# Attention in units of four query heads, with scores in turns on the two row halves of TensorE and values in turns on its two column halves

## What is computed

```python
def _sink_attend(q, k, v, bias, sinks):
    s = jnp.einsum('bnqhgd,bnkhd->bnhgqk', q, k).astype(jnp.float32) * (HEAD_DIM_A ** -0.5) + bias
    sink = sinks.astype(jnp.float32).reshape(N_KV_A, GROUP_A)[None, None, :, :, None, None]
    m = jnp.maximum(jnp.max(s, axis=-1, keepdims=True), sink)
    p = jnp.exp(s - m)
    p = p / (jnp.sum(p, axis=-1, keepdims=True) + jnp.exp(sink - m))
    return jnp.einsum('bnhgqk,bnkhd->bnqhgd', p.astype(v.dtype), v)
...
x += W_out( sigmoid(g_A) * SWA(h) + sigmoid(g_B) * GLA(h) ),  h = RMSNorm(x)
x += SwiGLU(RMSNorm(x))
```

## Time and profile before

| | |
|---|---|
| three runs | 994.55, 994.57 (median), 995.9 us |
| span of the profiled execution | 994.7 us |
| TensorE matmuls busy | 959.4 us (96%) |
| VectorE busy | 469.1 us (47%) |
| ScalarE busy | 352.6 us (35%) |
| GpSimd busy | 325.3 us (33%) |
| TensorE's granted clock, mean | 0.999 |
| from first scores to last values | 296 to 524 us |

### The profile page before, as it was taken

The page is one execution under the profiler, slowest core; times in us unless marked ns, Lnnn a source line. Parts: engine busy times, 40 slices in busy tenths (PEclk is TensorE's granted clock), DMA queues, the critical chain, the costliest instruction groups (busy, mean ns, idle before and its releaser), DMA issues.

```text
span 994.7 us, 17842 instructions
## 1 busy us (share of the span) xinstructions
PE 959.4 (96%) x7171; PEld 897.7 (90%) x7171; DVE 469.1 (47%) x970; ACT 352.6 (35%) x661; POOL 325.3 (33%) x139
## 2 busy tenths in 40 slices
PE   3999999999889999999999999999999999999997
PEld 3899999988878787878789999999999999999997
DVE  5673656647777557776755344222113222122321
ACT  5542433434444444344434443222112222122231
POOL 2442312122222112222323334443334444334450
PEclk9999999999999999999999999999999999999999
DMA  8332213231222211121115222223223223323212
GB/s 228 88 84 64 75 53 65 53 75 51 69 65 64 64 43 43 52 56 43 43 29 168 86 85 86 84 84 105 86 80 89 84 84 91 91 77 90 65 55 68
DMA packets 148787, 76.34 MB, mean 77 GB/s; under 512 B 19280, under 2 KB 147622, under 8 KB 148726
## 3 DMA queue, kind: packets, MB, share of 16 engines
q1 hardware_dynamic: 142582, 71.88, 25.9%
q10 hardware_dynamic: 6144, 3.61, 1.3%
HBM read 71.87 MB, written 3.60 MB: 76 GB/s over the span
## 4 chain that ended last, share of the span: by engine, by line
PE 82%; DVE 12%; ACT 3%; issue 2%; DMA 1%; SPq 0%; ACTq 0%; DVEq 0%
PE G L487 23%; PE G L489 22%; PE G L488 22%; PE X L650 3%; PE X L621 2%; DVE qAT L1315 2%; PE X L634 2%; DVE den L1354 1%; DVE rs L1118 1%; DVE rs L1117 1%; DVE rt L1119 1%; DVE rv L1280 1%; DMA xtok<-in_x_sample_dram 1%; PE X L580 1%; ACT rs L894 1%
## 5 line engine op out<-in xcount | busy, mean ns | idle before, releaser
L465 POOL TENSOR_TENSOR w_lo<-wraw,w_hi 128x1024 fp32r<-128x1024 f32 x129 | 323.6, 2508 | 645.3 <-ACT w_hi L807 645.2
L487 PE MATMUL G<-h_hi,w_hi 128*128 128x272 f32 x1280 | 382.7, 299 | 11.0 <-DVE rv L1280 8.6
L489 PE MATMUL G<-h_hi,w_lo 128*128 128x272 f32 x1280 | 371.0, 290 | 0.0
L488 PE MATMUL G<-h_lo,w_hi 128*128 128x272 f32 x1280 | 369.0, 288 | 0.0
L487 PEld LDWEIGHTS G<-h_hi,w_hi 128*128 128x128 f32 x1280 | 241.6, 189 | 30.7 <-issue 28.0
L488 PEld LDWEIGHTS G<-h_lo,w_hi 128*128 128x128 f32 x1280 | 242.0, 189 | 0.6
L489 PEld LDWEIGHTS G<-h_hi,w_lo 128*128 128x128 f32 x1280 | 241.5, 189 | 0.0
L487 PE MATMUL G<-f_hi,w_hi 128*128 128x272 f32 x704 | 203.0, 288 | 0.0
L489 PE MATMUL G<-f_hi,w_lo 128*128 128x272 f32 x704 | 202.9, 288 | 0.0
L488 PE MATMUL G<-f_lo,w_hi 128*128 128x272 f32 x704 | 202.1, 287 | 0.0
L807 ACT ACTIVATE w_hi<-wraw 128x1024 fp32r<-128x1024 f32 x129 | 135.3, 1049 | 89.1 <-PE G L489 89.1
(11 more groups left out here) (217 smaller groups left out, 968.7 us busy)
## 6 DMA issues: line engine op xcount, KB each, us to landing
wraw<-in_w_in_dram SPq DMA_DIRECT2D x45, 512.0 KB
wraw<-in_w_gate_dram SPq DMA_DIRECT2D x22, 512.0 KB
wraw<-in_w_up_dram SPq DMA_DIRECT2D x22, 512.0 KB
wraw<-in_w_down_dram SPq DMA_DIRECT2D x16, 512.0 KB
xtok<-in_x_prompt_dram SPq DMA_DIRECT2D x8, 512.0 KB, 5.2
wraw<-in_w_in_dram SPq DMA_DIRECT2D x16, 256.0 KB
wraw<-in_w_out_dram SPq DMA_DIRECT2D x8, 512.0 KB
wraw<-in_w_down_dram SPq DMA_DIRECT2D x8, 384.0 KB
```

The lines of the kernel that those rows point to most:

```text
L465: pool.tensor_tensor(w_lo[:, slot, :, :], wraw[:, slot, :, :], w_hi[:, slot, :, :].bitcast(F32), ALU.subtract).then_inc(w_split, 1)
L487: pe.matmul(o, w_hi[:, slot, kc, :], b_hi[:, kc, cols], start=(kc == 0), stop=False)
L488: pe.matmul(o, w_hi[:, slot, kc, :], b_lo[:, kc, cols], start=False, stop=False)
L489: mm = pe.matmul(o, w_lo[:, slot, kc, :], b_hi[:, kc, cols], start=False, stop=(kc == last))
```

## The change

- **Units.** 20 units (group, token tile) of four heads in place of 40 of two. qA tile i now holds heads 2i (partitions 0 to 63) and 2i + 1 (64 to 127), and its weights come in one DMA instead of two.
- **Key copies.** kST and kcS hold the keys with the two halves of the partitions exchanged. Four DMAs from SBUF to SBUF on ScalarE's queue make them in `keys_out`, behind the two outputs of keys; a new semaphore `k_swapped` holds the first unit back until they have landed.
- **Scores.** Four matmuls in turn on rows 0 to 63 and 64 to 127, even heads into XB[0], odd heads into XB[1]. The scores wait for the maximum of the unit just before (they waited for the one two before).
- **Turns and values.** In two parts a = 0, 1 of two heads each. Each values matmul has one head (128 columns), in turn into partitions 0 to 63 and 64 to 127 of XB[3].
- **Places.** Unit u belongs to tile UNIT0 + u, one tile for four heads as before. Behind chunk 0: values (u - 2, 1) and scores u. Behind chunk 3: turn (u - 1, 0). Behind chunk 6: values (u - 1, 0) and turn (u - 1, 1).
- **Other engines.** One slot per tile, ahead of `read_out` and `gates`. ScalarE: four exponentials of u, then both copies of u - 1. VectorE: unit_out(u - 2) over all 128 partitions, unit_max(u), unit_scale(u).

```diff
-    tiles += [("qA", 4 * u + i, [(O_QA + (8 * u + i) * HD, HD), (O_QA + (8 * u + 4 + i) * HD, HD)])
-              for u in range(2) for i in range(4)]
+    tiles += [("qA", i, [(O_QA + i * P, P)]) for i in range(KC)]
...
-UNITS = [(g, j, par) for g in range(KV_A) for j in range(NJ) for par in range(2)]
+GH = HEADS_A // KV_A
+UNITS = [(g, j) for g in range(KV_A) for j in range(NJ)]
 NU = len(UNITS)
-NB = 4
-LAG_T, LAG_V = 3, 4
+NB = 2
+LAG = 2
...
             def unit_scores(u):
-                g, j, par, heads, nq, lo, hi = unit_shape(u)
+                g, j, nq, lo, hi = unit_shape(u)
                 if u == 0:
                     pe.wait_ge(kt_out, 1)
+                    pe.wait_ge(k_swapped, 16 * 4)
                     pe.wait_ge(norm_done, len(NORMS))
-                if u >= 2:
-                    pe.wait_ge(smax_ok, u - 1)
-                hf = slice((g % 2) * HD, (g % 2) * HD + HD)
+                if u >= 1:
+                    pe.wait_ge(smax_ok, u)
                 t0 = TOK[j][0]
...
+                for a in range(2):
+                    for par in range(2):
+                        hf = slice(par * HD, (par + 1) * HD)
+                        keys, old = (kAT, kcT) if g % 2 == par else (kST, kcS)
+                        q = qAT[hf, 2 * g + a, t0:t0 + nq]
+                        o = XB[par][0:nq, a * 2 * P:(a + 1) * 2 * P]
...
+                            mm = pe.matmul(o[:, lo:hi], q, keys[hf, g // 2, t0 - P + lo:t0 - P + hi],
+                                           start=True, stop=True)
...
-            def unit_values(u):
...
+            def unit_values(u, a):
+                g, j, nq, lo, hi = unit_shape(u)
+                pe.wait_ge(pt_copied, 2 * u + a + 1)
+                if a == 0 and u >= 1:
                     pe.wait_ge(oa_ok, u)
...
-                    mm = pe.matmul(o, v, probT[0:nk, u % 2, :, kt, 0:nq], start=(kt == lo // P), stop=(kt == 1))
+                    for par in range(2):
+                        mm = pe.matmul(XB[3][par * HD:(par + 1) * HD, a * P:a * P + nq], v,
+                                       probT[0:nk, a, par, kt, 0:nq], start=(kt == lo // P), stop=(kt == 1))
...
-            for u in range(NU + LAG_V):
-                n, k = UNIT0 + u // 2, 3 + 4 * (u % 2)
+            for u in range(NU + LAG):
+                n = UNIT0 + u
+                if u >= LAG:
+                    put(n, 0, unit_values, u - LAG, 1)
                 if u < NU:
-                    put(n, k, unit_scores, u)
...
+                    put(n, 0, unit_scores, u)
+                if 1 <= u <= NU:
+                    put(n, 3, unit_turn, u - 1, 0)
+                    put(n, 6, unit_values, u - 1, 0)
+                    put(n, 6, unit_turn, u - 1, 1)
...
                 act.dma_start(nk_s[0, 0].rearrange("t h d -> t (h d)"), kout[0:DEC, 1, :]).then_inc(out_sem, 16)
+                for dst, src in ((kST, kAT), (kcS, kcT)):
+                    act.dma_start(dst[0:HD, :, :], src[HD:P, :, :]).then_inc(k_swapped, 16)
+                    act.dma_start(dst[HD:P, :, :], src[0:HD, :, :]).then_inc(k_swapped, 16)
...
             def slot(u):
 
-                if LAG_T <= u < NU + LAG_T:
-                    unit_copy(u - LAG_T)
                 if 0 <= u < NU:
                     unit_exp(u)
+                if 1 <= u <= NU:
+                    unit_copy(u - 1, 0)
+                    unit_copy(u - 1, 1)
...
-                if 1 <= u <= NU:
-                    unit_scale(u - 1)
+                if LAG <= u < NU + LAG:
+                    unit_out(u - LAG)
                 if 0 <= u < NU:
                     unit_max(u)
-                if LAG_V <= u < NU + LAG_V:
-                    unit_out(u - LAG_V)
+                    unit_scale(u)
```

More of the change, by code:

```diff
@@ L197, in mixer_program @@
         kcT = tensor(mix, "kcT", [P, 2, P])
+        kST = tensor(mix, "kST", [P, 2, T])
+        kcS = tensor(mix, "kcS", [P, 2, P])
         vA = tensor(mix, "vA", [P, NJ, KV_A * HD])
@@ L342, in mixer_program @@
         kt_out = sem("kt_out")
+        k_swapped = sem("k_swapped")
         out_sem = sem("out_sem")
@@ L613, in unit_scores @@
                 t0 = TOK[j][0]
-                for a, head in enumerate(heads):
-                    q = qAT[hf, 4 * (g // 2) + head % 4, t0:t0 + nq]
-                    o = XB[u % 2][0:nq, a * 2 * P:(a + 1) * 2 * P]
-                    if j == SJ:
-                        pe.matmul(o[:, 0:P], q, kcT[hf, g // 2, :], start=True, stop=True)
-                        mm = pe.matmul(o[:, P:P + DEC], q, kAT[hf, g // 2, SEQ:T], start=True, stop=True)
-                    else:
-                        mm = pe.matmul(o[:, lo:hi], q, kAT[hf, g // 2, t0 - P + lo:t0 - P + hi],
-                                       start=True, stop=True)
+                for a in range(2):
[4 more added lines that the diff above has]
+                        o = XB[par][0:nq, a * 2 * P:(a + 1) * 2 * P]
+                        if j == SJ:
+                            pe.matmul(o[:, 0:P], q, old[hf, g // 2, :], start=True, stop=True)
+                            mm = pe.matmul(o[:, P:P + DEC], q, keys[hf, g // 2, SEQ:T], start=True, stop=True)
+                        else:
+                            mm = pe.matmul(o[:, lo:hi], q, keys[hf, g // 2, t0 - P + lo:t0 - P + hi],
+                                           start=True, stop=True)
@@ L623, in unit_scores, with unit_turn @@
                 mm.then_inc(qk_done, 1)
-            def unit_turn(u):
-                g, j, par, heads, nq, lo, hi = unit_shape(u)
+            def unit_turn(u, a):
+                g, j, nq, lo, hi = unit_shape(u)
                 pe.wait_ge(prob_ok, u + 1)
-                if u >= 1:
-                    pe.wait_ge(pt_copied, u)
-                for a in range(2):
+                if 2 * u + a >= 1:
+                    pe.wait_ge(pt_copied, 2 * u + a)
+                for par in range(2):
@@ L1017, in _ @@
                     act.preload_act_table_set(EXP_TANH)
-                slot(2 * (n - UNIT0))
+                slot(n - UNIT0)
                 if n == N_IN - 1:
@@ L1032, in _ @@
                     high_part(n + RING)
-                slot(2 * (n - UNIT0) + 1)
                 for h in range(HEADS_B):
@@ L1355, in unit_scale @@
                 link(dve.reciprocal(rd[0:nq, s, :], den[0:nq, s, :]))
-                for a in range(2):
-                    o = prob[0:nq, s, a, lo:hi]
-                    ins = dve.tensor_scalar(o, o, rd[0:nq, s, a:a + 1], 0.5, ALU.mult, ALU.mult)
+                for i in range(GH):
+                    o = prob[0:nq, s, i, lo:hi]
+                    ins = dve.tensor_scalar(o, o, rd[0:nq, s, i:i + 1], 0.5, ALU.mult, ALU.mult)
                 ins.then_inc(prob_ok, 1)
             def unit_out(u):
-                g, j, par, heads, nq, lo, hi = unit_shape(u)
-                dve.wait_ge(pv_done, u + 1)
+                g, j, nq, lo, hi = unit_shape(u)
+                dve.wait_ge(pv_done, 2 * (u + 1))
                 for i in (2 * g, 2 * g + 1):
```

83 lines of the change are left out of this document (38 added, 45 removed).

## The result

The changed kernel takes 965.7 us (median of 4 runs, 964.3 to 966.7) against 994.6 for the kernel before beside it: a ratio of 0.9706, 95% interval 0.9692 to 0.9719. Forecast were 971.0 us, 967 to 985. The span, from which the forecast was added up, went from 994.7 to 964.8 us.

A forecast was written before the change was run, and what follows sets the result against it. TensorE, busy 96% of the span, was taken as the bound. Span 994.7 - 26.0 (two halves at once) + 2.3 (late first scores) + 1.8 (lower clock) - 1.8 (wait on unit_out gone) = 971.0 us, range 967 to 985.

The forecast's parts named there:

- the sign: Whole kernel: the change makes it faster, chance 0.89; same 0.03, slower 0.08.
- the full overlap of both kinds: TensorE's scores and values: both array halves work at once, halving 27.9 and 24.3 us of passes, together -26.0 us.
- the hole: TensorE ahead of the first scores: 3.6 us idle waiting for the query tile, +2.3 us.
- the fall of the clock: TensorE after the idle time ahead of the first scores: clock at 1.2 GHz for 3 to 6 us, +1.8 us.
- the end of the wait on gaT: TensorE's wait for VectorE's unit_out: gone since unit_out comes seven chunks ahead of the values needing it, -1.8 us.
- B: Scores and values: partial overlap, 8 passes take 5 steps and not 4, giving 977.5 us; chance 0.12.
- C: Scores and values: only one of the two kinds overlaps, giving 983 or 985 us; chance 0.15.
- E: Scores and values: each change of half costs a 0.09 us drain, no overlap, giving 1011.8 us; chance 0.08.
- the zero of the serial work: TensorE's attention blocks: without overlap, passes, changes of kind (8 a tile) and first weights cost the same, 0 us.
- The margin of 0.5 us: Values at chunk 6: probT's chain through VectorE and ScalarE takes 4.93 us, TensorE 5.43, so no wait.
- rival D: Values at chunk 6: full overlap, but probT late by 0.5 us in each of 20 units, giving 981 us; chance 0.10.
- The key copies: ScalarE's queue behind the keys' output: four issues of 0.45 us each, covered by a wait for VectorE, at most 0.5 us.

The follow-up runs named there:

- e5: Changed kernel with all four score matmuls of a unit reading queries and keys from rows 0 to 63: 979.5 us, ratio 0.9843.
- e6: Changed kernel with values matmuls head by head, all into output partitions 0 to 63: 980.2 us, ratio 0.9854.
- e1: Changed kernel with each unit's four score matmuls ordered half by half instead of in turns: 967.3 us, ratio 0.9720.
- e9: Changed kernel with the edits of e5 and e6 together, so neither scores nor values use two halves: 994.9 us, ratio 0.9997.
- e3: Kernel before with the turns first in each block, ahead of scores and values: 992.4 us, ratio 0.9967.
- e12: e11 with each unit's first turn (from the second unit) moved to chunk 0, between values and scores: 961.0 us, ratio 0.9661.
- e13: e11 with the same turn as in e12 moved to chunk 0, but ahead of the values: 960.0 us, ratio 0.9651.
- e10: Changed kernel with a unit's first turn behind chunk 1 and its copy ahead of the next unit's exponentials: 965.1 us, ratio 0.9693.
- e11: Changed kernel with the edits of e4, e8 and e10 combined (first unit's first turn stays behind chunk 3): 958.5 us, ratio 0.9631.
- e2: Changed kernel with the values matmuls of a part ordered column half by column half: 969.5 us, ratio 0.9743.
- e8: Changed kernel with the four key copies issued one in each of four tiles, not all in one: 965.1 us, ratio 0.9695.
- e4: Changed kernel with the first unit's scores behind chunk 5 of tile ga 1 instead of chunk 0: 965.3 us, ratio 0.9702.

## Why the prediction was off by 5 us

Right: the sign, the bound, the full overlap of both kinds (e5: 13.8 for 13.9; e6's full blocks: 12.0 for 12.1), the hole (3.56 us of wait for 3.6) and the fall of the clock with it, and the end of the wait on gaT. The price of the low clock was right in this kernel (1.9 us for 1.8), but by luck: worked out in the same way it is 1.6 us in e1 and 3.1 in e9, behind the same hole. Rivals B, C and E are out: no step of e5, e6 or e9 leaves room for a partial overlap or a drain at a change of half.

**The step that failed is the zero of the serial work**: "Changes of kind: before, two blocks a tile ..., 8 changes; after, ... 3 + 2 + 3 = 8". The cost of 0.09 us with late first weights, read off between scores and turns and between turns and values, is that of a change of the array shape, and I booked it for the way between projection and turns too. Counted by array shape a full weight tile had 8 changes (four in each of two blocks) and has 5: three around values and scores, two around values with turns, none around the turns alone. The turn block was forecast to take 0.80 us from projection to projection (0.22 + 0.38 + 0.20). It takes 0.49 (from the projection's start at 327.39 to the next one's at 327.88), and all that it adds is 0.44, which is 4 x 0.109. Three changes fewer are worth 0.50 us a full tile, 0.17 each; e3 and e12 against e13 give 0.14 to 0.15 for one. By the account below the term booked at 0 was worth -8.8 us.

I quoted the rule for this myself. The Trainium skill (TensorEngine Tiling (Array Packing), "Key Properties") says that a change of tiling mode drains TensorE and a change of tile alone doesn't. The trace agrees with it: halves change within 0.01 us, and each change of mode, which is what I call the array shape here, costs about 0.15. But I took kind for mode and never asked in which mode the turns stand. It is in each row of the profile, the 128*128 ahead of the moving operand's shape.

The account, against the span, from profiled executions. The first two terms are sums over all blocks of attention (44 before, 62 after) of what each adds, less the waits in them; the second also leaves out what the low clock adds to e9's first block (0.8 us) and e9's narrow order (3.5):

| term | forecast | measured | from |
|---|---|---|---|
| two halves at once | -26.0 | -26.3 | e9 against e10, sums of blocks |
| changes of the array shape | 0 | -8.8 | e9 against before, sums of blocks |
| hole ahead of the first scores | +2.3 | +2.3 | 3.56 us for 1.29 |
| clock at its lower level | +1.8 | +1.9 | tile ga 1 takes 12.46 us with the hole of 3.56, and 6.96 in e11 without it |
| key copies | 0 | +2.0 | 10.19 us for 8.21 to the start of the tile behind them |
| wait on gaT gone | -1.8 | -1.8 | waits |
| wait on probT at chunk 6 | 0 | +2.1 | sums of blocks, less e10's |
| start of the execution | 0 | -1.1 | second weight tile starts at 32.09 for 33.22 |
| sum | -23.7 | -29.7 | span: -29.9 |

The start is not the change's doing: the diff leaves the work there as it was, and in the profiled executions of the other variants of the changed kernel the second weight tile starts at 30.4 to 32.7 us. So the miss has one large term, which the forecast had at 0, and two costs of about 2 us each, also forecast at 0, that hid half of it.

**The margin of 0.5 us** at chunk 6 was named as rival D, and it happened in small: 11 waits of up to 0.5 us. I had weighed it against TensorE at its forecast pace; TensorE came 0.3 us sooner, since the turn block was that much shorter, and that took most of the margin. The rest can have gone on mx. I had it touch GpSimd's low part by 0.1 us and called that covered; it was held in 18 of 20 units, for up to 0.9 us. No run takes the two apart. D's price, 10 us, was far too high, as only some tiles miss it.

**The key copies** were priced by rows of another transfer, from SBUF to DRAM (0.45 us). The bound of 0.5 us was too low, they cost 2.0; a row for copies inside SBUF didn't exist.

The estimate from the figures of the Trainium skill for packed tiles (TensorE: Matmul & The Clock Gate, "Measured speedup vs the span model"), 1.59x for values and 1.54x for scores, gave 978 us. Measured is 2.0x for both: eight passes take four steps in place of eight, of 0.215 us for scores (e5) and 0.108 for values (e6). The measurement decides, for two halves of float32 with 256 and 128 columns.

## What to carry to other kernels

Group TensorE's work by the array shape, not by what the matmuls are for: read the rows*columns field along the queue, count its changes, and put transposes next to work on the whole array. Where two matmuls each need only half the array, alternate the halves, which doubled their pace here; four passes in a row on one half did no harm, eight did. When TensorE is the bound and is made faster, look first at the margins by which other engines were just in time: three repairs whose medians moved by some 0.5 us each alone gave 7.2 together.

## What the runs showed of the hardware that I had not expected

- Float32 matmuls on different halves start 0.007 us apart in both of their passes, and overlap in full, for rows as for columns.
- TensorE starts a pass for the other half while three passes of one half, queued ahead of it, have yet to start; with four or more it did not (e1).
- A group of narrow passes costs 0.23 us for each change of the array shape, whether it holds two or four of them (e2).
- An issue of a copy from SBUF to SBUF on ScalarE's queue grows from 0.53 to 1.60 us when four follow each other, and stays at 0.47 to 0.53 one a tile (e8).
- VectorE's small maximum of two SBUF operands ended with GpSimd's float32 operation, up to 1.08 us where it takes 0.16 alone.
- The granted clock was 0.50 by 294.4 us, 1.1 us after TensorE's last matmul ahead of the hole had ended (293.31), and until 301. Behind the same hole in e1 it was still 1.00 up to 296.8, 3.7 us after that matmul's end (293.09). In e13 it fell 1.5 us behind a wait of 1.6 us, and in e4 it did not fall with a wait of 2.5 us. So the length of one idle stretch did not tell whether it falls.
